# 128 tokens instead of 64 by gathered expert rows, one-hot rows in 2-byte token pairs, the last gates kept in SBUF

## The reference

```python
s1, i1 = lax.top_k(s[:, :, 0], 16); s2, i2 = lax.top_k(s[:, :, 1], 16)   # 8 heads, 128 + 128 keys
cand_s = s1[..., :, None] + s2[..., None, :]; cand_i = i1[..., :, None] * 128 + i2[..., None, :]
top_s, pos = lax.top_k(cand_s, 16); expert_idx = take(cand_i, pos); gate = softmax(top_s)
act = gelu(einsum("td,ted->te", x, u_tab[expert_idx]))     # 128 of 16384 experts for each token
y = einsum("te,ted->td", act * gate, v_tab[expert_idx])
```

## Time and profile before

| | |
|---|---|
| median of three runs | 2270.97 us |
| profiled execution, its own time | 2268.58 us |
| its span | 2266.8 us |
| PE busy | 2147.8 us (95%), 11716 matmuls |
| DVE, ACT, POOL busy | 1394.8, 842.3, 431.2 us |
| PE's mean granted clock | 0.986 |
| moved by DMA | 379.82 MB, 168 GB/s over the span |

### The profile page before, as it was taken

The page is one execution under the profiler, slowest core; times in us unless marked ns, Lnnn a source line. Parts: engine busy times, 40 slices in busy tenths (PEclk is TensorE's granted clock), DMA queues, the critical chain, the costliest instruction groups (busy, mean ns, idle before and its releaser), DMA issues.

```text
span 2266.8 us, 30308 instructions
## 1 busy us (share of the span) xinstructions
PE 2147.8 (95%) x11716; PEld 1841.2 (81%) x11716; DVE 1394.8 (62%) x2373; ACT 842.3 (37%) x1277; POOL 431.2 (19%) x539
## 2 busy tenths in 40 slices
PE   8988989889986999999999999999999999999999
PEld 8766666667664778889998999999998888999998
DVE  5442532532622653599996877785477776667776
ACT  4333432442442543233333555555332233233332
POOL 3132032041041100000000333331122221122221
PEclk9999999999998999999999999999999999999999
DMA  3210200200201632254543487878999998799886
GB/s 115 70 38 10 75 24 20 79 10 29 80 5 68 209 121 75 86 171 142 166 161 115 140 225 220 240 208 241 314 316 318 311 311 305 253 305 305 304 304 214
DMA packets 246526, 379.82 MB, mean 168 GB/s; under 512 B 130000, under 2 KB 179312, under 8 KB 246384
## 3 DMA queue, kind: packets, MB, share of 16 engines
q1 hardware_dynamic: 225968, 304.44, 41.4%
q0 software_dynamic: 20416, 73.44, 10.1%
HBM read 310.68 MB, written 67.11 MB: 167 GB/s over the span
## 4 chain that ended last, share of the span: by engine, by line
PE 63%; DVE 3%; ACT 0%; DMA 0%; issue 0%; SPq 0%; ACTq 0%
PE psE L84 20%; PE psE L85 20%; PE psE L86 20%; PE psE L1860 1%; PE psE L1861 1%; DVE expert_lo L1513 1%; DVE shared L1668 1%; PE psE L1820 1%; DVE shared L1588 1%; DMA raw<-in_w_mixers 0%; ACT expert_hi L1358 0%; DVE half_index L1592 0%; DVE shared L1597 0%; DVE top_position L1592 0%; DVE w_lo L1705 0%
## 5 line engine op out<-in xcount | busy, mean ns | idle before, releaser
L1513 DVE TENSOR_TENSOR expert_lo<-raw,expert_hi 128x1024 fp32r<-128x1024 f32 x288 | 352.1, 1223 | 251.7 <-ACT expert_hi L1358 249.0
L1358 ACT ACTIVATE expert_hi<-raw 128x1024 fp32r<-128x1024 f32 x288 | 305.4, 1061 | 531.3 <-PE psE L86 478.6
L84 PE MATMUL psE<-x2h,expert_hi 128*128 128x448 f32 x1024 | 379.9, 371 | 2.0 <-DVE expert_lo L1513 2.0
L84 PE MATMUL psE<-w_hi,expert_hi 128*128 128x448 f32 x1024 | 377.4, 369 | 3.3 <-DVE w_lo L1705 3.3
L86 PE MATMUL psE<-w_hi,expert_lo 128*128 128x448 f32 x1024 | 376.3, 367 | 0.0
L85 PE MATMUL psE<-w_lo,expert_hi 128*128 128x448 f32 x1024 | 376.2, 367 | 0.0
L86 PE MATMUL psE<-x2h,expert_lo 128*128 128x448 f32 x1024 | 374.3, 366 | 0.0
L85 PE MATMUL psE<-x2l,expert_hi 128*128 128x448 f32 x1024 | 374.3, 365 | 0.0
L84 PEld LDWEIGHTS psE<-w_hi,expert_hi 128*128 128x128 f32 x1024 | 192.2, 188 | 24.4 <-issue 5.7
L86 PEld LDWEIGHTS psE<-w_hi,expert_lo 128*128 128x128 f32 x1024 | 192.2, 188 | 18.5
L85 PEld LDWEIGHTS psE<-w_lo,expert_hi 128*128 128x128 f32 x1024 | 192.3, 188 | 18.2
(11 more groups left out here) (285 smaller groups left out, 3581.2 us busy)
## 6 DMA issues: line engine op xcount, KB each, us to landing
raw<-in_peer_u SPq DMA_DIRECT2D x128, 512.0 KB, 3.9
raw<-in_peer_v SPq DMA_DIRECT2D x128, 512.0 KB, 6.6
expert_acts<-gelu SPq DMA_DIRECT2D x128, 224.0 KB, 4.1
expert_gates<-shared SPq DMA_DIRECT2D x7, 4096.0 KB, 22.2
shared<-expert_acts SPq DMA_DIRECT2D x128, 224.0 KB, 4.0
shared<-expert_gates SPq DMA_DIRECT2D x128, 224.0 KB, 5.6
ring<-in_w_xonly SPq DMA_DIRECT2D x24, 512.0 KB, 3.3
ring<-in_w_full SPq DMA_DIRECT2D x16, 512.0 KB, 3.8
```

The costliest lines, as they stand in the source:

```text
L84: nc.tensor.matmul(out, sh, mh, start=first, stop=False)
L1358: nc.scalar.activation(wh[:, s % R, :], raw[:, s % R, :], ACT.Copy).then_inc(S["hi_done"], 1)
L1513: v.tensor_tensor(wl[:, s % R, :], raw[:, s % R, :], wh[:, s % R, :].bitcast(F32), ALU.subtract).then_inc(S["lo_done"], 1)
```

## The change

Now 128 tokens, in two groups of 64, go by gathered rows, and the dense part has 384. The 256 gathers are one list: dots of group 0, of group 1, adds of group 0, of group 1. The first 46 land in a ring of two slots and are used during the gates; the other 210 follow in the second half, one or two to a chunk. A route gets 16 chunks, so gates are made in chunks 64 to 111. One-hot rows hold pairs of tokens side by side, their columns are 2-byte values in SBUF (`cols`) instead of PSUM, and the fourth product moves from POOL to DVE. Five of the six blocks of gates are stored; the last stays in SBUF (`kept`). The first loads of `back` are put in another order.

```diff
@@ -91,13 +91,11 @@
-    c["iota"] = sb(ctx, "iota", [P, P], F16)
+    c["iota"] = sb(ctx, "iota", [P, 2 * P], F16)
@@ -712,7 +711,8 @@
-            turn(nc.vector.tensor_copy(c["iota"][:, :], c["iota_int"][:, :]))
+            turn(nc.vector.tensor_copy(c["iota"][:, :].rearrange("p (k t) -> p k t", t=2), c["iota_int"][:, :].rearrange(
+                "p (k t) -> p k t", t=1).broadcast_to([P, P, 2])))
@@ -1177,21 +1177,30 @@
-FEW = 64
-FOLD = P // FEW
-SLOTS = HK // FOLD
+GROUPS = ((0, 64), (64, 64))
+FEW = sum(count for _, count in GROUPS)
+FIRST_OPS = 46
 MANY = SEQ - FEW
 GATE_TOKENS = 8
-ROUTE_CHUNKS = 15
+ROUTE_CHUNKS = 16
 PAIRS_A = NT * ROUTE_CHUNKS
 PAIRS_B = MANY // GATE_TOKENS
 BLOCK = 64
-STORES = [len(range(b, MANY // BLOCK, 2)) for b in range(2)]
+PER_BLOCK = BLOCK // GATE_TOKENS
+BLOCKS = -(-MANY // BLOCK)
+SHIFT = (BLOCKS * BLOCK - MANY) // GATE_TOKENS
+STORED = MANY - BLOCK
+STORES = [len(range(b, BLOCKS - 1, 2)) for b in range(2)]
 HALF_ROWS = KEYS * BLOCK
+ROW_BANKS = (6, 0)
...
+GELU_AT = (24, 56)
 MIX, OUT, QUERY, U, V = 0, DC, 2 * DC, 4 * DC, 4 * DC + KEYS
...
-        xh, xl = sb("x2h", [P, DC, SEQ], F32R), sb("x2l", [P, DC, SEQ], F32R)
...
+        xh, xl = sb("x2h", [P, DC, MANY], F32R), sb("x2l", [P, DC, MANY], F32R)
+        rows_x = [sb(f"few_rows{g}", [P, D]) for g in range(len(GROUPS))]
...
-        mh, ml = sb("w_hi", [P, 2, MANY], F32R), sb("w_lo", [P, 2, MANY], F32R)
...
-        first, second, high, low16 = (sb(name, [P, 2, GATE_TOKENS, KEYS], F16)
-                                      for name in ("first_hot", "second_hot", "second_hi", "second_lo"))
+        with ExitStack() as first_half:
+            u_ring = c["sb"](first_half, "u_gathered", [P, 2, D])
+        mh, ml = (sb(name, [P, 2, SEQ], F32R)[:, :, 0:MANY] for name in ("w_hi", "w_lo"))
+        with ExitStack() as second_half:
+            few_ring = c["sb"](second_half, "few_gathered", [P, R, D])
+        hots = [sb(name, [P, 2, GATE_TOKENS // 2, KEYS, 2], F16) for name in ("first_hot", "second_hot", "second_hi",
+                                                                             "second_lo")]
...
-        few_ring = shared[:, 8 * SEQ:8 * SEQ + R * D].rearrange("p (r d) -> p r d", d=D)
...
+        kept = rows[(BLOCKS - 1) % 2]
+        free = (BLOCKS % 2) * HALF_ROWS
...
+        few_ops = [(table, g, m) for table in "uv" for g, (_, count) in enumerate(GROUPS) for m in range(count)]
@@ -1306,9 +1328,10 @@
-                sp.wait_ge(S["gates_moved"], 2 * (BLOCK // GATE_TOKENS) * (b + 1))
-                sp.dma_start(gates_dram[:, :, b * BLOCK:(b + 1) * BLOCK].rearrange("j i t -> i j t"),
-                             rows[b % 2]).then_inc(rows_stored[b % 2], 16)
+                sp.wait_ge(S["gates_moved"], 2 * (PER_BLOCK * (b + 1) - SHIFT))
+                t0, t1 = max(b * BLOCK - SHIFT * GATE_TOKENS, 0), (b + 1) * BLOCK - SHIFT * GATE_TOKENS
+                sp.dma_start(gates_dram[:, :, t0:t1].rearrange("j i t -> i j t"),
+                             rows[b % 2][:, :, BLOCK - (t1 - t0):]).then_inc(rows_stored[b % 2], 16)
@@ -1321,13 +1344,11 @@
             load(0)
             for k in range(DC):
                 sp.dma_start(mixer_out[:, k, :], mixed[k]).then_inc(mixed_loaded[k], 16)
-                if k % 4 == 3:
-                    load(k // 4 + 1)
-            load(3)
+            for r in range(1, R):
+                load(r)
...
@@ -1405,6 +1426,8 @@
                 act.wait_ge(S["weighted"], j + 1)
+                if j == 0:
+                    act.wait_ge(S["few_used"], FIRST_OPS)
                 if j >= 2:
@@ -1440,8 +1462,9 @@
                     act.wait_ge(S["rows_turned"], DC)
-                    nc.scalar.activation(rows_x[:, :], ps[:, 6:8, :].rearrange("p b d -> p (b d)"),
-                                         ACT.Copy).then_inc(S["rows_copied"], 1)
+                    for g, b in enumerate(ROW_BANKS):
+                        nc.scalar.activation(rows_x[g][:, :], ps[:, b:b + 2, :].rearrange("p b d -> p (b d)"),
+                                             ACT.Copy).then_inc(S["rows_copied"], 1)
@@ -1460,23 +1483,28 @@
                     split_w(j + 1)
-                if j == 60:
-                    act.wait_ge(S["few_dots"], SLOTS)
-                    nc.scalar.activation(few_act[:, :], few_act[:, :], ACT.Gelu).then_inc(S["few_gelu"], 1)
+                if j in GELU_AT:
+                    g = GELU_AT.index(j)
+                    act.wait_ge(S["few_used"], few_done("u", g))
+                    nc.scalar.activation(few_act[g][:, :], few_act[g][:, :], ACT.Gelu).then_inc(S["few_gelu"], 1)
...
+            def gather(n):
+                table, g, m = few_ops[n]
+                source = u_rows if table == "u" else v_dram.rearrange("j i d -> (j i) d")
+                k = n - FIRST_OPS
+                if k < 0:
+                    ring, slots, landed, ahead = u_ring, 2, u_gathered, n
+                else:
+                    ring, slots, landed, ahead = few_ring, R, gathered, k
+                r = ahead % slots
+                if ahead >= slots:
+                    pool.wait_ge(S["few_used"], n - slots + 1)
+                pool.indirect_dma_start(ring[:, r, :], None, source,
+                                        bass.IndirectOffsetOnAxis(ap=which[g][:, m:m + 1], axis=0)).then_inc(landed[r], 16)
+
+            pool.wait_ge(S["mixed_hi"], DC - 2)
@@ -1487,22 +1515,17 @@
             pool.wait_ge(S["few_picked"], 2)
-            for f in range(1, FOLD):
-                for part in (which, few_gate):
-                    pool.dma_start(part[f * FEW:(f + 1) * FEW, 0:SLOTS],
-                                   part[0:FEW, f * SLOTS:(f + 1) * SLOTS]).then_inc(few_spread, 16)
-            pool.wait_ge(few_spread, 32 * (FOLD - 1))
-            for p in range(PAIRS_B):
-                pool.wait_ge(S["hot_ready"], 2 * p + 1)
-                t0 = FEW + p * GATE_TOKENS
-                part = rest[:, t0:t0 + GATE_TOKENS].rearrange("p (t a) -> p t a", a=1).broadcast_to(
-                    [P, GATE_TOKENS, KEYS])
-                nc.gpsimd.tensor_tensor(low16[:, p % 2, :, :], second[:, p % 2, :, :], part,
-                                        ALU.mult).then_inc(S["low_ready"], 1)
-            for b in range(2):
-                pool.wait_ge(rows_stored[b], 16 * STORES[b])
-            for m in range(2 * SLOTS):
-                gather(m)
+            for g, (t0, count) in enumerate(GROUPS):
+                for f in range(P // count):
+                    for out_, in_ in ((which[g], picked_expert), (few_gate[g], picked_gate)):
+                        pool.dma_start(out_[f * count:(f + 1) * count, :],
+                                       in_[t0:t0 + count, f * count:(f + 1) * count]).then_inc(few_spread, 16)
+            pool.wait_ge(few_spread, 16 * SPREADS)
+            for n in range(FIRST_OPS):
+                gather(n)
+            pool.wait_ge(S["gates_made"], 2 * PAIRS_B)
+            for n in range(FIRST_OPS, len(few_ops)):
+                gather(n)
@@ -1600,10 +1623,11 @@
                 tokens = slice(i * P, (i + 1) * P)
-                v.tensor_scalar(part16[:, :], ps[:, 2, tokens], 4096.0, None, ALU.mult)
+                v.tensor_copy(cols[:, 0, tokens], ps[:, 0, tokens])
+                v.tensor_copy(cols[:, 1, tokens], ps[:, 1, tokens])
+                v.tensor_scalar(cols[:, 2, tokens], ps[:, 2, tokens], 4096.0, None, ALU.mult)
                 step(v.tensor_scalar(whole, ps[:, 2, tokens], 4096.0, None, ALU.mult))
-                v.tensor_copy(ps[:, 3, tokens], part16[:, :])
...
+                v.tensor_tensor(cols[:, 3, tokens], whole, cols[:, 2, tokens], ALU.subtract).then_inc(S["taken"], 1)
                 dve.wait_ge(S["taken"], i + 1)
@@ -1653,64 +1677,88 @@
                 low_next()
+                low_next()
                 step(v.reciprocal(total[:, :], total[:, :]))
...
+            def few_first(n):
+                dve.wait_ge(u_gathered[n % 2], 16 * (n // 2 + 1))
+                few_dot(n, u_ring, n % 2)
+
+            def few_next(k):
+                dve.wait_ge(gathered[k % R], 16 * (k // R + 1))
+                (few_dot if few_last[k][0] == "u" else few_add)(FIRST_OPS + k, few_ring, k % R)
+
...
-                grid = [P, GATE_TOKENS, KEYS]
-                keys = c["iota"][:, :].rearrange("p (a k) -> p a k", a=1).broadcast_to(grid)
-                col = lambda k: ps[:, k, tokens].rearrange("p (t a) -> p t a", a=1).broadcast_to(grid)
-                v.tensor_tensor(second[:, p % 2, :, :], keys, col(1), ALU.is_equal).then_inc(S["hot_ready"], 1)
-                v.tensor_tensor(first[:, p % 2, :, :], keys, col(0), ALU.is_equal).then_inc(S["hot_ready"], 1)
+                grid = [P, GATE_TOKENS // 2, KEYS, 2]
+                keys = c["iota"][:, :].rearrange("p (a k t) -> p a k t", a=1, t=2).broadcast_to(grid)
+                col = lambda k: cols[:, k, tokens].rearrange("p (a b t) -> p a b t", b=1, t=2).broadcast_to(grid)
```

(55 more changed lines are left out.)

110 lines of the change are left out of this document (57 added, 53 removed).

## The result

The changed kernel takes 2240.48 us (median of 4 runs, 2238.29 to 2244.28) against 2270.88 for the kernel before on the same chip: ratio 0.9858, interval 0.9827 to 0.989, or 30 us less. I had forecast 2204, 67 us less, in a range of 2168 to 2256. The sign is right and the time lies in the range, but outside the 2180 to 2228 that had 60%, and less than half of the forecast gain came. Two executions of the study, one of 3066 us of the repaired kernel before and one of 6149 us of the kernel before, were in a slow state and enter no ratio.

A forecast was written before the change was run, and what follows sets the result against it. PE was taken to bound both expert halves, with DVE pacing routing and the DVE chain close behind late. Routing -1, gates -59 and second half -6 gave -66 us, a median of 2204 us, range 2168 to 2256.

The forecast's parts named there:

- Ahead of the experts: Before the expert stage: 16 more `turn_rows` matmuls cost 1.8 us; shifted transfers taken as 0, bounds -4 and +3.
- Routing: While tokens are routed: DVE sets the pace, 72.2 us a route; gates(0) starts near 1242; -1 us.
- Gates: First gates to second half: 310.7 us plus 12 for late stores, against 381.4 before; -59 us.
- Second half: `outputs` half of the expert stage: 626 us against 632, including +9 for late gathers; -6 us.
- chain term: Second half: ACT split, DVE low half, gathered rows, low half of weighted acts hold 127 chunks at 617 us.
- The rule: Second half: two consecutive chunks take at least 9.9 us if the later has two gathered rows; averages 4.73 or 4.95.
- Last chunk: End of the kernel: 16 short fold matmuls in place of 8 lie beside the final adds, 0 us.
- Rival 2: Transfers run at 346 GB/s: second half +14 us, gates +33 in place of +12, total time 2239 us; chance 17%.
- Rival 3: Transfers already at their limit, 315 GB/s: second half +78 us, gates +28, total time 2310 us; chance 7%.
- Rival 1: No double rate on DVE among the gates: 6.85 us a chunk, +69 us, 2273, no change; chance 8%.
- Rival 4: Strided one-hots slow PE among the gates: +46 us, total time 2250 us; chance 4%.
- Rival 5: Chain looser and transfers keep up: second half at PE's 4.25 us a chunk, 540 us, total 2118; chance 4%.

The follow-up runs named there:

- the repaired kernel before: Kernel before, with stores of gate rows on ACT's queue and the low half of weighted acts ahead of gathered rows: 2257.52 us, ratio 0.9945.
- the best version: Changed kernel, row stores on ACT's queue, low half before gathered rows, 26 of 210 rows moved behind the gates: 2116.29 us, ratio 0.9333.

## Why the prediction was right and wrong

**Matmuls**: right, 4.16 us for 4.20. **Ahead of the experts**: the traces start the first half anywhere between 933.0 and 944.4 us, before and after, so neither the forecast +1.8 nor the measured +2.8 can be told from that spread.

**Routing**: right. Routes are 72.4, 71.9 and 71.9 us long (forecast 72.2), and gates(0) starts at 1242.94 (1242).

**Gates**: this is the step that failed, in the sentence "Two to three us late per store of five: **+12**, bounds 0 and 35". It measured 42, 8.4 a store, outside the bounds. I had the place (SP's queue behind a store) but took the acts for what waits there, "in a ring of four, which lasts five chunks", 25.8 us. The load of weights stands in the same queue, and it has 17.5 us of slack from a free slot to the split that ACT must make before the move that PE waits for; it took 24.8. That split stands ahead of the move in ACT's order, a path that the forecast did not look at. Of the 42, about 25 are there without gathers, since the slack fell from 20.8 to 17.5, and 17 come from the gathers, which lengthen the hold from 16.4 to 19.8 us. The trace of before had the warning, ACT's six waits for these loads. The rest of the step stands: 5.16 us a chunk, one-hots at 0.61 from start to start, next to no cost of the strided operand. With the stores moved, first gates to second half takes 312.7 us; I had 310.7 without the +12. My estimate of the delay by the engines' capacity (45 us of work in 41) was the wrong kind of sum: the engines did carry more, 328 GB/s, once nothing stood in the queue.

**Second half**: right in its mechanism and near in size, 626 forecast, 632.8 in the profiled execution and 626.8 to 628.1 in three others with the same code there. The chain term was 617 for 618.4, and that closeness is luck. The rule as stated gives less: 210/128 makes about 108 chunks at its 4.73 us and 20 at its 4.95, which is 605 us for 127 chunks and not 617. In the pattern one, two, two of dots a chunk takes 4.72 on average, as the rule has it; in that of adds 4.92, as two adds in a row take 2.67 us where I counted 2 x 1.20 plus the 0.08 of a start, and the second waits for the first. That is about what the rule lacks, 13 us. The check on the kernel before proves little too: with PE's own 4.86 us the rule gives 623 (127 x 4.86, and 0.8 more for each of seven two-row chunks) for the measured 632, and the rest is the wider spacing of matmuls, which I had taken for PE's pace ("4.86 to 4.96").

**Last chunk**: forecast 0, measured +2.2. Sixteen fold matmuls in place of eight don't hide: the chunk takes 7.11 us against its 4.17 where no row is late, and 6.16 against 4.86 before, so 1.6 us more; the late last rows add 1.0, the final adds 0.3, and the chunk itself is 0.7 shorter.

**Rivals.** Rival 2 (346 GB/s) gives 2239, and 2240 was measured, but for another reason: it put 33 us into the gates and 14 into the second half by a rate that four runs exceed. It is refuted, and a time that fits a rival does not show it. That the measured time lies in my range is as little a merit: a stop of the right place and wrong size fell into it. Rival 3 falls with it. Rival 1 is what the token-by-token layout does. Rival 4 is refuted. Rival 5's premise was wrong for the order of the change, but its second half of 540 us is what the best version reaches with another order.

What stays open: why a load of 512 KB behind the store is held at issue so long when the store itself takes 0.43 us to issue. Whether smaller stores on SP's queue would do was not tried, nor the move ahead of the split in ACT's order, which would take PE off this path with the stores where they are.

## What to carry to other kernels

When an engine's chunk gets shorter, every ring shrinks in time: for each queue with a long transfer in it, list everything behind that transfer, and hold each one's slack, in the new chunk time, against the hold plus landing. Read the slack from a trace and not from the number of slots: it ends where the bound engine needs anything that stands behind the late item in the order of the engine that waits for it. Waits of an engine that isn't the bound, like ACT's six, show which slack is nearly gone. Put rare long transfers on a queue with nothing behind them. On an engine that feeds the bound, do what the bound waits for first and the rest after it; what that is worth can't be read from the wait alone: here waits of 80 us stood for 60, and then transfers were the limit.

## What the hardware showed that I had not expected

- A 4096 KB store of 256-byte pieces on its own queue takes 38.4 us to land beside loads and gathers, and disturbs neither: loads of 512 KB land in 4.6 us (median), at 328 GB/s in all.
- Loads and gathers together sustain 384 to 395 GB/s for hundreds of us, at a DMA share of 1.00 to 1.03. A share of 0.97 at 352 GB/s still had a tenth in it.
- For a two-operand DVE instruction on 2-byte values in SBUF, the innermost step decides: pairs in steps of one element run at 0.61 us for 1024 elements, a repeated single value at 1.14.
- After 7.3 us of idle time PE came back at half its clock for about 4 us.
- Behind a wait of PE, matmuls of 384 columns start 0.177 us apart (median of 84 chunks of the second half) and not 0.1735 (the 42 others); in the kernel before, 0.2067 in place of 0.2027 lasts for many chunks.
